# A hybrid attention and mixture-of-experts step: score halves on 64 rows, sampled value products on column groups in turn, page multiplies behind the weight difference

## The chip, the cores and the metric

The kernel runs on one core of one Trainium2 chip. Its time is the device time of one execution in microseconds (us); the metric is the median over the runs. The core has a matrix engine (TensorE, PE in the profile; PEld are its weight loads), VectorE (DVE), ScalarE (ACT), GpSimd (POOL) and SyncE (SP), which here only issues transfers.

## What is computed

One decoder layer over 256 prompt positions and 8 sampled sequences of one token each. Everything is fp32. Cut to what matters here:

```
q, k, v, bg, cg, xc = split(rms_norm(x) @ w_in)        # q, k: 8 heads x 2 halves x 64; v: 8 heads x 128
# prompt, per head h; c is the half of q and k
s[c] = (q[c] . k[c]) * 64**-0.5 - slope[h] * dist       # causal
a = softmax(s[0]) - lam * softmax(s[1]);  o = a @ v     # "the weight difference", then the value product
# sampled tokens: the same against 256 past keys and values, read by page_table (2 pages of 128 x 1024 each)
y_conv = bg * conv3(cg * xc)
x += [rms_norm(o) * (1 - lam_init) | y_conv] @ w_out
x += top-2 experts of 32 (SwiGLU, 2048 -> 512 -> 2048)
```

## The kernel before

**Stages.** First the normed input is multiplied with `w_in` in 48 output tiles of 128 columns (`tile(n)`, 16 products of 128x128 by 128x264 each, L603), then 16 tiles of `w_out`, then the router, then 8 groups of 4 experts. Tile order: 8 of q, 8 of k, 8 of v (n = 0 to 23), then C, X and B of the convolution in turn (n = 24 + 3i is C, + 1 is X, + 2 is B, for i = 0 to 7). Tile n writes PSUM bank n % 3.

**The attention steps lie between the tiles on PE.** Head h has its scores behind tile 18 + 3h (`head_scores`), its three transposes behind tile 19 + 3h (`head_turn`, L652 to L654, which waits for the semaphore `diffed`), its value products behind tile 20 + 3h (`head_pv`). Between scores and transposes stands one tile. In that time DVE adds the bias (`bias_scores`, L1142, L1145), takes the maxima, ACT the exponentials, DVE the output of the head before (`head_out`, L1134) and the difference of the two softmaxes (`difference`, L1157 to L1163), whose last operation counts `diffed` up.

**Scores.** POOL copies the two 64-row halves of q into `qz`, a tile whose other halves are zero (`split_q`, L1454 and L1456), so that each half can be multiplied with all 128 rows of k. `head_scores` then does per half one product of 256 and one of 128 columns, the long ones into bank 5, the short ones into bank 6.

**Sampled tokens.** The key pages are read into the ring (units `KP`, four pages of 512 KB), POOL multiplies each page with the broadcast q (`multiply_page`, L1468, units `QB` hold q), DVE sums it up (`page`, L1129) behind `conv_output(i)`. `PAGES_AT = [3, 3, 3, 3, 2, 2, 0, 0]` says how many pages belong to convolution step i. The value pages (units `VP`, again four pages each) are multiplied behind tile 44 (`sample_pv`, L692), with 32 columns of weights each, so that sample b writes the 32 rows of column group b % 4 of banks 4 and 5.

**Transfers.** `ring` has 8 slots of 2 MB. SP issues the units of `FRONT` in that list's order, each after the work on the unit that held its slot 8 units ago. Near the end of the list stand ("X", 3), ("B", 3), four VP units and eight W units (`w_out`). ("B", 3) takes the slot of the second QB unit and so waits for all 16 page multiplies (`page_mul`); the VP units stand behind it in SP's queue. Behind W come the experts' weights, 12 MB an expert.

**DVE and POOL** both work in SBUF on their own queues, each in program order.

Of the kernel before, what the change touches and what calls it, by code (L numbers as in the profile page):

```python
# [15 lines left out]
ALU = mybir.AluOpType  # L16
# [3 lines left out]
P = 128  # L20
D = 2048
KT = D // P
SEQ = 256
NB = 8
T = SEQ + NB
TT = 3
H = 8
HD = 128
HALF = HD // 2
ATT = H * HD  # L30
CONV = D - ATT
CT = CONV // P
PAST = 256
PAGE = 128
NPG = PAST // PAGE
# [17 lines left out]
C = P // EG  # L53
# [21 lines left out]
BCX = 3 * H  # L75

PAGES_AT = [3, 3, 3, 3, 2, 2, 0, 0]
PAGES_BY = [sum(PAGES_AT[:i]) for i in range(CT + 1)]
NPAGES = NB * NPG
NIN = BCX + 3 * CT  # L80
HEAD0 = 2 * H + 2
# [47 lines left out]
def build(nc, ins, outs):  # L129
    ctx = ExitStack()  # L130
    with ctx:
# [3 lines left out]
        def sem(name):  # L135
            return ctx.enter_context(nc.semaphore(name))

        ring = sb("ring", [P, SLOTS, UNIT])
# [11 lines left out]
        bank = [ctx.enter_context(nc.psum_tensor(f"bank{i}", [P, 512], F32)) for i in range(8)]  # L150
# [19 lines left out]
        qkT = bc[:, KT * T:].rearrange("p (k t) -> p k t", t=T)  # L170
        vrow = xa[:, 0, :].rearrange("p (t c) -> p t c", t=2)
        qrows = xa[0:NB, 0, 0:ATT]
        tmp = xa[:, 1:3, :].rearrange("p a n -> p (a n)")
        prob = tmp[:, 0:768]
        qz = tmp[:, 768:1280].rearrange("p (c q) -> p c q", c=2)
        osq = tmp[:, 1296:1552]
        ord_ = tmp[:, 1560:1816]
        sq = [tmp[:, 1296 + T * i:1296 + T * i + T] for i in range(2)]
# [11 lines left out]
        pairw = tmp[:, 0:512].rearrange("p (g b c) -> p g b c", g=NPG, b=NB)  # L190
# [114 lines left out]
        qk_ready = sem("qk_ready")  # L305
# [9 lines left out]
        stash_T = sem("stash_T")  # L315
        stash_out = sem("stash_out")
        stash_ready = sem("stash_ready")
        qz_ready = sem("qz_ready")
        qz_zero = sem("qz_zero")
        scores = sem("scores")  # L320
        biased = sem("biased")
        exped = sem("exped")
        diffed = sem("diffed")
# [7 lines left out]
        page_mul = sem("page_mul")  # L331
# [8 lines left out]
        s_pv = sem("s_pv")  # L340
# [49 lines left out]
        front_at = {}  # L390
# [155 lines left out]
        def _(pe):  # L546
# [86 lines left out]

            def head_scores(h):

                pe.wait_ge(qz_ready, h + 1)
                if h >= 1:
                    pe.wait_ge(biased, h)
                for c in range(2):
                    pe.matmul(bank[5][:, c * SEQ:(c + 1) * SEQ], qz[:, c, P:SEQ], qkT[:, H + h, 0:SEQ],  # L640
                              start=True, stop=True)
                for c in range(2):
                    m = pe.matmul(bank[6][:, c * P:(c + 1) * P], qz[:, c, 0:P], qkT[:, H + h, 0:P],
                                  start=True, stop=True)
                m.then_inc(scores, 1)

            def head_turn(h):
# [33 lines left out]
            def sample_pv():  # L681

                pe.wait_ge(s_pair_copied, 2)
                pe.wait_ge(rows_out, 3 * H)
                for b in range(NB):
                    u = b // 2
                    if b % 2 == 0:
                        arrived(pe, ("VP", u))
                    for g in range(NPG):
                        page = ((b % 2) * NPG + g) * ATT  # L690
                        for half in range(2):
                            m = pe.matmul(bank[4 + half][C * (b % 4):C * (b % 4 + 1), :], pairw[:, g, b, :],  # L692
                                          ring[:, front_at[("VP", u)][0], page + half * 512:page + (half + 1) * 512],
                                          start=b < 4 and g == 0, stop=b >= 4 and g == NPG - 1, skip_group_check=True)
                    if b % 2:
                        m.then_inc(s_pv, 1)

            def sample_pick():

# [12 lines left out]
            for n in range(NIN):  # L712
# [5 lines left out]
                h, stage = divmod(n - HEAD0, 3)  # L718
# [357 lines left out]
        def _(dve):  # L1076
# [61 lines left out]
            def bias_scores(i):  # L1138

                dve.wait_ge(scores, i + 1)  # L1140
                for c in range(2):
                    st.add(V.scalar_tensor_tensor(prob[:, c * SEQ:(c + 1) * SEQ], const("dist"), SLOPES[i],  # L1142
                                                  bank[5][:, c * SEQ:(c + 1) * SEQ], ALU.mult, ALU.add))
                for c in range(2):
                    st.add(V.scalar_tensor_tensor(prob[:, 512 + c * P:512 + (c + 1) * P], const("dist")[:, P:2 * P], SLOPES[i],  # L1145
                                                  bank[6][:, c * P:(c + 1) * P], ALU.mult, ALU.add))
                st.wait()
                st.do(V.tensor_reduce(nmax[:, 0:2], prob[:, 0:512].rearrange("p (c k) -> p c k", c=2), AX.X, ALU.max, negate=True))
                V.tensor_reduce(nmax[:, 2:4], prob[:, 512:768].rearrange("p (c k) -> p c k", c=2), AX.X, ALU.max, negate=True
                                ).then_inc(biased, 1)  # L1150
# [284 lines left out]
        @block.gpsimd  # L1435
        def _(pool):
            G = nc.gpsimd
            G.memset(xa[:, 2, :], 0.0).then_inc(x_clear, 1)
            pool.wait_ge(x_clear, 1)
            xs = ins["x_sample"].rearrange("b o d -> b (o d)")  # L1440
            pool.dma_start(xa[0:NB, 2, :], xs).then_inc(x_in[2], 16)

            pool.dma_start(outs["conv_sample"][0, :, 0, :], ins["state_conv"][0, :, 1, :]).then_inc(state_stored, 16)


            pool.wait_ge(h_T, KT)
            G.memset(qz, 0.0).then_inc(qz_zero, 1)
            pool.wait_ge(qz_zero, 1)
            def split_q(h):
                pool.wait_ge(qk_ready, h + 1)  # L1450
                if h >= 1:
                    pool.wait_ge(scores, h)

                G.tensor_copy(qz[0:HALF, 0, :], qkT[0:HALF, h, 0:SEQ]).then_inc(qz_zero, 1)  # L1454
                pool.wait_ge(qz_zero, h + 2)
                G.tensor_copy(qz[HALF:P, 1, :], qkT[HALF:P, h, 0:SEQ]).then_inc(qz_ready, 1)  # L1456
                pool.wait_ge(qz_ready, h + 1)

            def multiply_page(j):
                b = j // NPG  # L1460
                if j % PPU == 0:
                    arrived(pool, ("KP", j // PPU))
                if b % 4 == 0 and j % NPG == 0:
                    arrived(pool, ("QB", b // 4))
                s, _ = front_at[("KP", j // PPU)]
                sq_, _ = front_at[("QB", b // 4)]
                kp = ring[:, s, (j % PPU) * ATT:(j % PPU + 1) * ATT]
                G.tensor_tensor(kp, kp, ring[:, sq_, (b % 4) * ATT:(b % 4 + 1) * ATT], ALU.mult).then_inc(page_mul, 1)  # L1468

            for n in range(HEAD0 - 3, NIN, 3):  # L1470

                h, i = (n + 3 - HEAD0) // 3, (n - BCX) // 3
                if h < H:
                    split_q(h)
                if i >= 0:
                    for j in range(PAGES_BY[i], PAGES_BY[i + 1]):
                        multiply_page(j)
                    if PAGES_AT[i]:
                        pool.wait_ge(page_mul, PAGES_BY[i + 1])

            pool.wait_ge(scores, H)
            pool.wait_ge(self_ready, 1)
            G.memset(wrv, 0.0).then_inc(wr_zero, 1)
            G.memset(rbias, FAR).then_inc(wr_zero, 1)
            pool.wait_ge(wr_zero, 2)
            pool.dma_start(wrv[:, :, 0:GROUPS], ins["w_router_group"].rearrange("l (k p) e -> (l p) k e", p=P)).then_inc(wr_in, 16)
            pool.dma_start(wrv[:, :, RG:], ins["w_router_expert"].rearrange("l (k p) e -> (l p) k e", p=P)).then_inc(wr_in, 16)
            pool.dma_start(rbias[:, 0:GROUPS], ins["b_router_group"].partition_broadcast(P).rearrange("p l e -> p (l e)")  # L1490
                           ).then_inc(wr_in, 16)
            pool.dma_start(rbias[:, RG:], ins["b_router_expert"].partition_broadcast(P).rearrange("p l e -> p (l e)")
                           ).then_inc(wr_in, 16)
            pool.wait_ge(wr_in, 64)
            G.tensor_tensor(wrv, wrv, gffnT.unsqueeze(2).to_broadcast([P, KT, RE]), ALU.mult).then_inc(wr_ready, 1)

            pool.wait_ge(o_ready, H + 1)
            G.memset(xa[:, 2, :], 0.0).then_inc(x2_zero, 1)
            pool.dma_start(consts[:, late0:late0 + 512], ins["late"]).then_inc(late_in, 16)

            pool.wait_ge(tile_done, NIN)
            G.memset(h2[:, 2, :], 0.0).then_inc(h2_zero, 1)
            pool.wait_ge(h2_zero, 1)
            for j in range(KT):
                pool.wait_ge(y_added, j + 1)
                cols = slice(j * P, (j + 1) * P)
                G.tensor_copy(h2[:, 0:2, cols], xa[:, 0:2, cols]).then_inc(h2_ready, 1)
                G.tensor_copy(h2[0:NB, 2, cols], xa[0:NB, 2, cols]).then_inc(h2_ready, 1)
# [64 lines left out]
```

## Time and profile before

| | before |
|---|---|
| time, median of 3 runs | 1541.65 us (1540.58 to 1541.82) |
| span of the profiled execution | 1537.7 us |
| what the runs' median has beyond that span | 3.95 us |
| PE busy | 1353.1 us (88%) |
| DVE, ACT, POOL busy | 375.5, 213.2, 67.2 us |
| read from HBM | 496.35 MB |

The span is from the first to the last instruction of one profiled execution. For that execution no time of its own is given beside its span, so the 3.95 us are the difference of two executions. Busy shares are means over stages with different limits.

### The profile page before, as it was taken

How to read it: one execution, taken by the hardware profiler on the slowest of the kernel's cores; microseconds unless marked ns; L12 is line 12 of the kernel's file. 1: busy time of each engine (PE TensorE's matmuls, PEld its weight loads, DVE VectorE, ACT ScalarE, POOL GpSimd, SP SyncE). 2: the span in 40 equal slices, each digit the busy share in tenths (PEclk: the TensorE clock that was granted, in tenths of full speed). 3: DMA queues.
4: the chain of work that ended last, by engine and by line, in shares of the span. 5: the costliest groups of instructions: out<-in, count | busy, mean ns of one | idle time of the engine just before them, and what ended most of it. 6: DMA issues, size and time to landing. Idle time of an engine off the chain costs nothing.

```text
span 1537.7 us, 19543 instructions
## 1 busy us (share of the span) xinstructions
PE 1353.1 (88%) x8104; PEld 912.7 (59%) x8104; DVE 375.5 (24%) x842; ACT 213.2 (14%) x555; POOL 67.2 (4%) x82
## 2 busy tenths in 40 slices
PE   6999999989999987879969879879879878978887
PEld 5888888778687766436426437436535535535542
DVE  3322144644111123113103103203113113112112
ACT  4111231212001120110100100100110110110110
POOL 0000022421010000000000000000000000000000
PEclk9999999989999998879979979889989989988988
DMA  9964334757197432999999999999999999999997
GB/s 299 353 202 175 128 127 144 244 178 243 50 313 268 154 120 101 417 424 423 420 423 423 423 418 424 424 419 422 423 422 418 425 423 418 422 424 422 418 426 294
DMA packets 135644, 503.39 MB, mean 327 GB/s; under 512 B 6214, under 2 KB 80638, under 8 KB 118702
## 3 DMA queue, kind: packets, MB, share of 16 engines
q1 hardware_dynamic: 125670, 495.25, 81.3%
q10 hardware_dynamic: 9600, 6.95, 1.4%
q0 software_dynamic: 336, 0.67, 0.2%
q8 instruction: 26, 0.43, 0.1%
q14 instruction: 12, 0.10, 0.0%
HBM read 496.35 MB, written 6.53 MB: 327 GB/s over the span
## 4 chain that ended last, share of the span: by engine, by line
PE 70%; DMA 17%; DVE 5%; SPq 5%; issue 2%; ACT 1%; ACTq 0%; DVEq 0%
PE bank L603 28%; DMA ring<-in_w_up 13%; PE bank L811 11%; PE bank L798 9%; PE bank L870 7%; PE bank L849 5%; SPq L485 4%; PE bank L834 4%; DMA ring<-in_w_down 2%; DVE bc L1415 1%; PE bank L692 1%; DVE xa L1161 1%; DVE cat L1410 1%; PE bank L754 1%; DMA ring<-in_w_in 1%
## 5 line engine op out<-in xcount | busy, mean ns | idle before, releaser
L603 PE MATMUL bank<-bc,ring 128*128 128x264 f32 x1536 | 353.9, 389 | 1.7 <-DMA ring<-in_w_in 1.7
L798 PE MATMUL bank<-ring,cat 128*32 128x512 f32 x2048 | 270.9, 661 | 82.0 <-DMA ring<-in_w_gate 37.7
L603 PEld LDWEIGHTS bank<-bc,ring 128*128 128x128 f32 x1536 | 290.9, 192 | 52.2 <-DMA ring<-in_w_in 1.9
L870 PE MATMUL bank<-ring,bc 128*32 128x256 f32 x2048 | 174.7, 512 | 33.9 <-DVE bc L1417 28.7
L798 PEld LDWEIGHTS bank<-ring,cat 128*32 128x32 f32 x2048 | 62.1, 116 | 225.6 <-issue 120.1
L811 PEld LDWEIGHTS bank<-bc 128*128 128x128 f32 x768 | 169.4, 311 | 15.1 <-issue 14.1
L849 PEld LDWEIGHTS bank<-consts,bc 128*128 128x128 f32 x512 | 124.3, 327 | 90.3 <-DVE bc L1415 61.0
L811 PE MATMUL bank<-bc 128*128 128x128 f32 x768 | 170.4, 383 | 5.6 <-DVE bc L1379 5.6
L849 PE MATMUL bank<-consts,bc 128*128 128x32 f32 x512 | 131.5, 401 | 26.0 <-DVE bc L1415 26.0
L870 PEld LDWEIGHTS bank<-ring,bc 128*32 128x32 f32 x2048 | 84.8, 144 | 112.1 <-issue 82.1
L603 PE MATMUL bank<-cat,ring 128*128 128x264 f32 x512 | 117.9, 389 | 0.0
L603 PEld LDWEIGHTS bank<-cat,ring 128*128 128x128 f32 x512 | 96.0, 190 | 21.5 <-issue 5.9
L1415 DVE COPY bc<-bank 128x512 f32<-128x512 f32 x32 | 22.1, 692 | 349.2 <-PE bank L798 349.2
L1425 DVE COPY cat<-bank 32x256 f32<-32x256 f32 x128 | 54.3, 424 | 164.3 <-PE bank L870 162.3
L1071 ACT ACTIVATE cat<-bank 32x256 f32<-32x256 f32 x128 | 47.9, 374 | 177.6 <-PE bank L870 176.0
L1410 DVE TENSOR_TENSOR cat<-bank,gains 128x512 f32<-128x512 f32 x32 | 22.1, 692 | 154.1 <-PE bank L811 154.1
L834 PE MATMUL bank<-cat,bc 128*128 128x512 f32 x128 | 59.2, 605 | 0.0
L1431 DVE TENSOR_TENSOR xa<-xa,bank 128x512 f32<-128x512 f32 x72 | 49.5, 688 | 14.7 <-PE bank L834 10.9
L1116 DVE RECIPROCAL xa<-xa 128x264 f32<-128x264 f32 x16 | 28.8, 1803 | 89.9 <-ACT xa L923 89.9
L1064 ACT ACTIVATE bc<-bank 128x128 f32<-128x128 f32 x32 | 8.9, 278 | 288.6 <-PE bank L849 288.6
L834 PEld LDWEIGHTS bank<-cat,bc 128*128 128x128 f32 x128 | 23.0, 189 | 33.0 <-issue 26.3
L1059 ACT ACTIVATE bc<-bank 128x384 f32<-128x384 f32 x8 | 3.9, 491 | 262.3 <-PE bank L822 262.3
(239 smaller groups left out, 640.9 us busy)
## 6 DMA issues: line engine op xcount, KB each, us to landing
ring<-in_w_gate SPq DMA_DIRECT2D x64, 2048.0 KB, 23.6
ring<-in_w_up SPq DMA_DIRECT2D x64, 2048.0 KB, 23.1
ring<-in_w_down SPq DMA_DIRECT2D x64, 2048.0 KB, 27.6
ring<-in_w_in SPq DMA_DIRECT2D x24, 2048.0 KB, 10.6
ring<-in_w_out SPq DMA_DIRECT2D x8, 2048.0 KB, 17.1
ring<-in_cache_k SPq DMA_DIRECT2D x16, 512.0 KB, 4.6
ring<-in_cache_v SPq DMA_DIRECT2D x16, 512.0 KB, 5.3
ring<-qrows_scratch SPq DMA_DIRECT2D x2, 2048.0 KB, 7.3
```

Of the source, the lines that this page charges most:

```text
L485: sp.dma_start(ring[:, s, :], src).then_inc(slot_full[s], 16)
L603: m = pe.matmul(bank[n % 3][:, 0:T], w[:, k, (i % TPU) * P:(i % TPU + 1) * P], src[:, k, :], start=n_k == 0, stop=n_k == KT - 1)
L798: m = pe.matmul(bank[b][c * C:(c + 1) * C, :], xeT[:, 8 * i + k, j * C:(j + 1) * C], w[:, k, :], start=i == 0 and k < 4, stop=i == 1 and k ...
L811: m = pe.matmul(bank[4 + q % 2][:, (k % 4) * P:(k % 4 + 1) * P], h2[:, t, k::KT], sel[:, t, :], start=t == 0, stop=t == TT - 1)
L834: m = pe.matmul(to[:, :], gateT[:, t, :], ye[:, n * 512:(n + 1) * 512], start=True, stop=True)
L849: m = pe.matmul(bank[3][:, (x * FC + c) * C:(x * FC + c + 1) * C], src[:, c::FC], const("fold"), start=True, stop=True)
L870: m = pe.matmul(bank[2 + 2 * i][n * C:(n + 1) * C, 0:256], actT[:, c, :], w[:, c, n, :], start=c == 0, stop=c == FC - 1, skip_group_check= ...
L1071: A(ye[j * C:(j + 1) * C, i * 1024 + n * 256:i * 1024 + (n + 1) * 256], bank[2 + 2 * i][n * C:(n + 1) * C, 0:256], ACT.Copy).then_inc(ye_a ...
L1410: V.tensor_tensor(xeT[:, 4 * q:4 * q + 4, :], bank[4 + q % 2][:, :].rearrange("p (k s) -> p k s", k=4), gffn[:, 4 * q:4 * q + 4].unsqueeze ...
L1415: V.tensor_copy(u_sb, bank[1][:, :]).then_inc(u_copied, 1)
L1425: V.tensor_copy(ye[j * C:(j + 1) * C, i * 1024 + n * 256:i * 1024 + (n + 1) * 256], bank[2 + 2 * i][n * C:(n + 1) * C, 0:256]).then_inc(ye ...
L1431: V.tensor_tensor(xa[:, t, cols], xa[:, t, cols], bank[5 + x % 3][:, :], ALU.add).then_inc(mix_added, 1)
```

## The change

Three edits. In `head_scores` the padded `qz` is gone: each half of q and k is multiplied with its own 64 rows, half c into bank 5 + c (256 columns for the second block of positions, then 128 for the first); POOL's `memset` and 16 copies go with it. In `sample_pv` the samples go in two rounds of four; within a round, page and half are the outer loops and the four samples, hence the four column groups, the inner one; PE waits for two VP units ahead of each round. POOL's page multiplies of step i wait for `diffed` of head i + 2 (at most head 7), where they stood behind `split_q(i + 3)`, which waited for the scores of head i + 2.

```diff
             def head_scores(h):
 
-                pe.wait_ge(qz_ready, h + 1)
+                pe.wait_ge(qk_ready, H + h + 1)
                 if h >= 1:
                     pe.wait_ge(biased, h)
-                for c in range(2):
-                    pe.matmul(bank[5][:, c * SEQ:(c + 1) * SEQ], qz[:, c, P:SEQ], qkT[:, H + h, 0:SEQ],
-                              start=True, stop=True)
-                for c in range(2):
-                    m = pe.matmul(bank[6][:, c * P:(c + 1) * P], qz[:, c, 0:P], qkT[:, H + h, 0:P],
-                                  start=True, stop=True)
+                for q0, q1, b0 in ((P, SEQ, 0), (0, P, SEQ)):
+                    for c in range(2):
+                        half = slice(c * HALF, (c + 1) * HALF)
+                        m = pe.matmul(bank[5 + c][:, b0:b0 + q1], qkT[half, h, q0:q1], qkT[half, H + h, 0:q1],
+                                      start=True, stop=True)
                 m.then_inc(scores, 1)
...
                 pe.wait_ge(rows_out, 3 * H)
-                for b in range(NB):
-                    u = b // 2
-                    if b % 2 == 0:
+                for r in range(2):
+                    for u in (2 * r, 2 * r + 1):
                         arrived(pe, ("VP", u))
                     for g in range(NPG):
-                        page = ((b % 2) * NPG + g) * ATT
                         for half in range(2):
-                            m = pe.matmul(bank[4 + half][C * (b % 4):C * (b % 4 + 1), :], pairw[:, g, b, :],
-                                          ring[:, front_at[("VP", u)][0], page + half * 512:page + (half + 1) * 512],
-                                          start=b < 4 and g == 0, stop=b >= 4 and g == NPG - 1, skip_group_check=True)
-                    if b % 2:
-                        m.then_inc(s_pv, 1)
+                            for x in range(4):
+                                b = 4 * r + x
+                                page = ((b % 2) * NPG + g) * ATT + half * 512
+                                m = pe.matmul(bank[4 + half][C * x:C * (x + 1), :], pairw[:, g, b, :],
+                                              ring[:, front_at[("VP", b // 2)][0], page:page + 512],
+                                              start=r == 0 and g == 0, stop=r == 1 and g == NPG - 1, skip_group_check=True)
+                    m.then_inc(s_pv, 2)
...
-            for n in range(HEAD0 - 3, NIN, 3):
-
-                h, i = (n + 3 - HEAD0) // 3, (n - BCX) // 3
-                if h < H:
-                    split_q(h)
-                if i >= 0:
+            for i in range(CT):
+                if PAGES_AT[i]:
+
+                    pool.wait_ge(diffed, min(i + (BCX - HEAD0) // 3, H - 1) + 1)
                     for j in range(PAGES_BY[i], PAGES_BY[i + 1]):
                         multiply_page(j)
-                    if PAGES_AT[i]:
-                        pool.wait_ge(page_mul, PAGES_BY[i + 1])
+                    pool.wait_ge(page_mul, PAGES_BY[i + 1])
```

On POOL, before, the last copies of q (head 7), the last four page multiplies and the clearing of the router's weights stand so:

```order
L1454 COPY xa<-bc 64x256 [waits scores,qk_ready,page_mul]
L1456 COPY xa<-bc 64x256 [waits qz_zero]
L1468 TENSOR_TENSOR ring<-ring 128x1024 [waits slot_full2,qz_ready]
L1468 TENSOR_TENSOR ring<-ring 128x1024
L1468 TENSOR_TENSOR ring<-ring 128x1024 [waits page_mul]
L1468 TENSOR_TENSOR ring<-ring 128x1024
L1485 MEMSET bc 128x640 [waits self_ready,scores,page_mul]
```

At the same place of the changed kernel:

```order
L1452 TENSOR_TENSOR ring<-ring 128x1024 [waits slot_full2,diffed,page_mul]
L1452 TENSOR_TENSOR ring<-ring 128x1024
L1452 TENSOR_TENSOR ring<-ring 128x1024 [waits diffed,page_mul]
L1452 TENSOR_TENSOR ring<-ring 128x1024
L1466 MEMSET bc 128x640 [waits self_ready,scores,page_mul]
```

All four used to follow the scores of head 6; now the first two follow the difference of head 6 and the last two that of head 7, and the router's clearing stays behind them.

On PE, before, the sampled value products of the first two samples and the first wait of the next two (one row is one product; a product of fp32 is two instructions in the trace):

```order
L692 MATMUL bank4<-ring,xa 32x512 [waits slot_full6,rows_out,s_pair_copied]
L692 MATMUL bank5<-ring,xa 32x512
L692 MATMUL bank4<-ring,xa 32x512
L692 MATMUL bank5<-ring,xa 32x512
L692 MATMUL bank4<-ring,xa 32x512
L692 MATMUL bank5<-ring,xa 32x512
L692 MATMUL bank4<-ring,xa 32x512
L692 MATMUL bank5<-ring,xa 32x512
L692 MATMUL bank4<-ring,xa 32x512 [waits slot_full7]
```

The same stage of the changed kernel, first round and start of the second:

```order
L689 MATMUL bank4<-ring,xa 32x512 [waits slot_full6,slot_full7,rows_out,s_pair_copied]
L689 MATMUL bank4<-ring,xa 32x512 x3
L689 MATMUL bank5<-ring,xa 32x512 x4
L689 MATMUL bank4<-ring,xa 32x512 x4
L689 MATMUL bank5<-ring,xa 32x512 x4
L689 MATMUL bank4<-ring,xa 32x512 [waits slot_full1,slot_full0]
```

Four products with the same bank in a row are those of the four column groups. The last two units (slots 0 and 1) are now waited for together, ahead of the whole second round.

## Rows read from the trace of the kernel before

**Rows 1.** The page, section 2: granted TensorE clock in 40 slices of 38.4 us

```profile
PEclk9999999989999998879979979889989989988988
```

**Rows 2.** Busy time by stretch: us, PE, PEld, DVE, ACT, POOL, PEclk, DMA share, GB/s

```profile
500.00:550.00 50.00, 50.00 (x226) 39.50 (x226) 7.17 (x26) 5.93 (x36) 3.78 (x12) 1.00 0.36 131
700.00:800.00 100.00, 83.34 (x601) 49.72 (x601) 15.24 (x39) 9.38 (x21) 0.00 (x0) 0.90 1.01 421
```

**Rows 3.** The chain that ended last, 272 to 348 us: start, us, what

```profile
272.33 0.75 DVE xa L1142 x2
...
298.55 0.75 DVE xa L1142 x2
...
304.43 2.30 DVE xa L1161
...
308.10 8.81 PE bank L603 x32
...
326.47 0.75 DVE xa L1142 x2
...
338.41 9.26 PE bank L603 x32
```

**Rows 4.** Timeline, 296 to 345 us: start, us, engine line op

```profile
299.61 7.02 POOL L1468 TENSOR_TENSOR ring<-ring 128x1024 f32<-128x1024 f32 x3
...
317.30 3.47 DVE L1129 TENSOR_REDUCE xa<-ring 128x16 f32<-128x1024 f32 x3
...
327.52 9.39 POOL L1468 TENSOR_TENSOR ring<-ring 128x1024 f32<-128x1024 f32 x4
...
334.73 2.46 DVE L1162 SCALAR_TENSOR_TENSOR xa<-xa,small 128x256 f32<-128x256 f32 x1
```

**Rows 5.** Timeline of head 7, for which POOL multiplies no page

```profile
357.22 0.75 DVE L1142 SCALAR_TENSOR_TENSOR xa<-consts,bank 128x256 f32<-128x256 f32 x2 [6.83 <-PE bank L643]
...
362.61 0.28 DVE L1161 TENSOR_SCALAR xa<-xa,small 128x128 f32<-128x128 f32 x1
...
363.32 0.35 DVE L1163 SCALAR_TENSOR_TENSOR xa<-xa,small 128x128 f32<-128x128 f32 x1
364.14 0.27 PE L652 MATMUL bank<-consts,xa 128*128 128x128 f32 x1
```

**Rows 6.** Groups by line, 160 to 425 us: busy, mean ns, idle before

```profile
L652 PE MATMUL bank<-consts,xa 128*128 128x128 f32 x8 | 2.7, 333 | 11.3 <-DVE xa L1163 11.3
```

**Rows 7.** The same chain, 355 to 418 us

```profile
355.87 0.86 PE bank L640 x4
356.74 0.45 PE bank L643 x4
357.18 7.12 PE bank L603 x32
...
379.53 0.43 PE bank L632 x2
...
395.31 15.78 PE bank L692 x64
411.09 7.32 PE bank L603 x32
```

**Rows 8.** The same chain, among the experts

```profile
624.81 5.15 PE bank L798 x48
```

**Rows 9.** Timeline of SP's queue, 336 to 376 us

```profile
336.94 0.37 SPq L473 DMA_DIRECT2D ring<-in_w_in  x1
338.07 38.02 SPq L468 DMA_DIRECT2D ring<-in_cache_v  x16
```

**Rows 10.** Issues at 342.1, 358.4 and 359.5 us: KB, us to landing

```profile
ring<-in_cache_v SPq DMA_DIRECT2D x1, 512.0 KB, 8.0
...
ring<-in_cache_v SPq DMA_DIRECT2D x1, 512.0 KB, 5.1
...
ring<-in_cache_v SPq DMA_DIRECT2D x1, 512.0 KB, 8.5
```

More of the change, by code:

```diff
@@ L174, in build @@
         prob = tmp[:, 0:768]
-        qz = tmp[:, 768:1280].rearrange("p (c q) -> p c q", c=2)
         osq = tmp[:, 1296:1552]
@@ L317, in build @@
         stash_ready = sem("stash_ready")
-        qz_ready = sem("qz_ready")
-        qz_zero = sem("qz_zero")
         scores = sem("scores")
@@ L1142, in bias_scores @@
                     st.add(V.scalar_tensor_tensor(prob[:, c * SEQ:(c + 1) * SEQ], const("dist"), SLOPES[i],
-                                                  bank[5][:, c * SEQ:(c + 1) * SEQ], ALU.mult, ALU.add))
+                                                  bank[5 + c][:, 0:SEQ], ALU.mult, ALU.add))
                 for c in range(2):
                     st.add(V.scalar_tensor_tensor(prob[:, 512 + c * P:512 + (c + 1) * P], const("dist")[:, P:2 * P], SLOPES[i],
-                                                  bank[6][:, c * P:(c + 1) * P], ALU.mult, ALU.add))
+                                                  bank[5 + c][:, SEQ:SEQ + P], ALU.mult, ALU.add))
                 st.wait()
@@ L1446, in _ @@
             pool.wait_ge(h_T, KT)
[L1447 to L1457, printed above, removed]
             def multiply_page(j):
```

## The prediction

> **What bounds the kernel now.** I read the busy time by stretch first, then the chain of waits, then the timeline of one head with page multiplies and of one without. Late in the program the transfers bound it: from 700 to 800 us the DMA share is 1.01 at 421 GB/s. From 500 to 550 us, while `w_out` is multiplied, PE is busy for all 50 us and the DMA share is 0.36 [rows 2]: the ring is full of expert weights, and the stream goes on only when the first experts free slots. The chain up to there runs through PE. So what PE (or what PE waits for) saves ahead of the experts starts the saturated stream earlier by as much, and I count it in full.
>
> In that front part the chain leaves PE once per head: PE has done the tile behind the scores and waits at L652 for DVE's last operation of the difference, 11.3 us in all [rows 6]. The reader should set two heads side by side. In the head at 298.55, POOL multiplies three pages from 299.61 to 306.6, and DVE's small L1161 takes 2.30 us in the chain [rows 3, 4]. In head 7 POOL multiplies none, L1161 takes 0.28, and from the first bias (357.22) to the end of L1163 (363.67) DVE needs 6.45 us; PE's tile takes 7.12, and L652 starts at 364.14 without a wait [rows 5, 7]. The last head with pages has four of them, and there L1162 takes 2.46 too [rows 4]. So some DVE operations stand still until a page multiply (2.34 to 2.35 us each, 7.02 over 3 and 9.39 over 4) is done.
>
> **Page multiplies behind the difference.** The distance of one head's scores from the next is 26.22 us at 272.33, 27.92 at 298.55 and 30.75 at 326.47 (to 357.22) [rows 3, 5]; the two heads before repeat the first. Without pages it is 24.09: from 357.18 to the end of the sums at 379.96, plus the 1.31 us of scores [rows 7]. Five heads: 3 x 2.13 + 3.83 + 6.66 = 16.9, less 0.3 for transposes of v that one of them has between its tiles: 16.5 us. Part of it is clock: after the waits at heads 5 and 6 a tile took 8.81 and 9.26 us where 7.12 is usual [rows 3, 7], in the slice where the page shows 8 tenths [rows 1]; 3.8 of the 16.5 hang on that, and they come back only if PE no longer idles. DVE has then 0.4 us to spare per head (363.67 against 364.14), so this term rests on a thin cover.
>
> What is late instead: the multiplies now lie over DVE's convolution step, which can be held until the last of three is done, 7.1 us after the difference, or 6.45 + 7.1 = 13.6 us after the scores, plus the operations themselves, some 2 us more. The product with B needs its tile anyhow, two tiles of 7.12 and 0.3 of transposes, 14.6 us after the scores. With the multiplies' end at 15.6, 0.4 for that product and 3.5 for the page sums (3.47 us for three [rows 4]) DVE is free 19.5 us after the scores, and the next scores come at 23.7. Cost 0; without this cover every us beyond the spare 4.2 would be paid once per head.
>
> **The moved transfers.** This is the price. All 16 multiplies used to be done 10 us after the scores of head 6 (at 336.9), and ("B", 3) was issued at 336.94 with the 16 value pages behind it [rows 4, 9]. Now the last two wait for head 7: 6.45 + 2 x 2.35 = 11.2 us after its scores; counted from the old 357.2 that is 368.4, 31.5 us later than 336.94. POOL's router loads wait behind them and fall into the same stretch. When are the value pages wanted? The products started 38.1 us after head 7's scores (357.18 to 395.31) [rows 7]; the second round begins 3.5 us later, so the last pages are due 41.6 - 11.2 = 30.4 us after ("B", 3) is issued. Before, the fourth page, issued at 342.1, landed 8.0 later [rows 10], 13.2 after that issue with 4.2 MB moved. Twelve pages (6.3 MB) more take 15.0 us at 421 GB/s [rows 2] or 19.8 at the pace of those 13.2: 28.2 to 33.0. The router's loads cost a page 8.5 against 5.1 us when they were issued beside it [rows 10], so 3.4 more: 31.6 to 36.4, a wait of 1.2 to 6.0 us. I take 3, nearer the quick end since a queue that never runs dry should hold its pace, and 1 more for the clock, about half of the 2.1 us that the tile at 338.41 lost. Cost 4. ("B", 3) itself is due at tile 44, some 20 us after its issue, and lands in time.
>
> **Value products in turn.** Now 64 instructions take 15.78 us, 247 ns each [rows 7]: one column group gets eight in a row, and only neighbours overlap. The experts' L798 has the new order with the same shape: 48 in 5.15 us, 107 ns each [rows 8]. So 64 x 0.107 = 6.9, with 0.2 for the start 7.1: 8.7 saved.
>
> The Trainium skill ("TensorE: Matmul & The Clock Gate", Part 3, what overlaps and what doesn't) has matmuls start and end in strict program order. With the two passes of each fp32 product adjacent, that allows only one overlap per neighbouring pair and would leave this stage near 14 us. The trace speaks against it, since L798 could not then reach 107 ns.
>
> **Scores on 64 rows.** Now 0.86 + 0.45 = 1.31 us per head [rows 7]. The new products have the same columns, twice 256 and twice 128. Side by side on the two row halves they take half, 0.65; one after the other 1.31. No row of this trace shows a product on 64 rows. To this comes the change of array shape, twice a head: the tile behind the 32-column stage took 7.32 instead of 7.12 [rows 7], so 0.2 for one change; I take 0.3 for the two. Bounds: 0.36 saved per head, or 0.3 lost. The nearest rows are the column groups, which do run side by side, so I take the gain: 8 x 0.36 = 2.9 saved, the other end being 2.4 lost. POOL's copies stood beside other work and PE never waited for them: 0.
>
> The skill's page "TensorEngine Tiling (Array Packing)" (Key Properties) says that changing the tiling mode drains TensorE, and that tiles work independently. The 0.2 us of the trace are what such a drain costs here; by that page the sum would be the same.
>
> **Sum.** 16.5 + 8.7 + 2.9 - 4 = 24.1. The span goes from 1537.7 to 1513.6; with the 3.95 us that the median has beyond it, 1517.5.
>
> **Rivals.**
> - No wait for the value pages (0.25): the queue holds 421 GB/s and the router's loads cost less than 3.4. 28.1 saved, 1513.5. For it: the quick bound misses by only 1.2 us.
> - Row halves in sequence, with the wait (0.16): 24.1 - 5.3 = 18.8, 1522.8. For it: no row shows them side by side.
> - A long wait for the pages, 6 us and a slow clock behind it (0.08): about 9 for 4, 19, 1522.5; at the far end 1526. For it: the slow pace in [rows 10].
> - Products in program order (0.04): the value stage saves 1.7, the scores 0.16 a head, which is 1.3, and with the second round so much later the pages are in time: 16.5 + 1.7 + 1.3 = 19.5, 1522.1. This is the rule of the skill named above. Against it: [rows 8].
> - The port wait isn't POOL's doing and stays (0.02): 16.5 fall away and the pages' lateness too; the rest, with serial row halves, is 8.7 - 2.4 = 6.3, 1535. Against it: head 7.
> - Slower (0.03): DVE, held in the convolution step, is late for the next head's bias. Place: five heads. Price: 1 us per head and us beyond the spare 4.2. It takes back all 28.1 us only from 4.2 + 28.1 / 5 = 9.8 us of extra hold on; three multiplies are 7.1 us. At 12 us it gives 1541.65 - 28.1 + 5 x 7.8 = 1552.5.
> - What is left, 0.42, is the forecast.
>
> **How the numbers follow.** 1517.5 is the likeliest case. Its own uncertainty is the wait (0 to 9) and the 0.2 us per change of shape. The range, 1510 to 1526, holds the forecast, no wait and the three cases near 1522; the low end is no wait with cheaper changes of shape, 30.5 saved being 1511. A run can tell 0.2% or 3 us from no change, and all but the last two cases are beyond that: faster 0.95, same 0.02, slower 0.03.
>
> **What would show it.** In the profile after: L1161 at 0.28 us in all heads and no idle time before the transposes; distances between scores of 23.7 us; no tile at 8.8 or 9.3 us there; the value products near 7 us with a gap of about 3 us in their middle that ends with a DMA of `cache_v`; the eight score groups at 0.65 to 0.7 us and the tile behind each some 0.2 longer; held DVE operations in L1174 to L1178 instead. A wait before ("B", 3)'s tile, a gap of more than 9 us among the value products, or idle time that stays before the transposes would make the prediction wrong.

## The result, and the profile after

| | before | changed |
|---|---|---|
| time, median of 4 runs | 1541.12 us (1540.55 to 1541.82) | 1517.74 us (1515.57 to 1518.75) |
| span of the profiled execution | 1537.7 us | 1515.5 us |
| that execution's own time | not given | 1517.3 us |
| PE busy | 1353.1 us | 1340.8 us |
| DVE, POOL busy | 375.5, 67.2 us | 388.9, 60.4 us |

The ratio is 0.9847, with a 95% interval from 0.9835 to 0.986: the changed kernel is 1.5% faster, 23.4 us by the medians and 22.2 us by the spans.

The chain that ended last, in the changed kernel (start, us, what), answers to [rows 3] and [rows 7]. L639 is the 64-row scores, L648 the first transpose, L600 the tiles, L689 the sampled value products.

```profile
243.40 7.32 PE bank L600 x32
250.72 0.11 PE bank L648
...
267.23 7.32 PE bank L600 x32
...
337.86 0.88 PE bank L639 x8
338.76 0.75 DVE xa L1138 x2
...
347.68 2.40 POOL ring L1452
350.10 0.37 SPq L470
...
369.02 14.61 DMA ring<-in_cache_v
383.63 0.14 issue
383.77 5.34 PE bank L689 x32
389.11 7.32 PE bank L600 x32
```

Where DVE stood between scores and transposes of the heads with pages, the chain now runs from tile to transpose without leaving PE. Behind head 7's scores it leaves PE by another way: through DVE's bias and difference, the last page multiplies on POOL (L1452), the issue of ("B", 3) (L470) and of the value pages behind it, to the landing of the last page, for which the second round of value products waits. The scores come every 23.83 us (243.40 to 267.23) where it was 26.22 to 30.75. Head 7's scores are done at 338.76, 18.4 us earlier than at 357.18, and the tile behind the value products starts at 389.11 instead of 411.09: 22.0 us. The span's gain is 22.2, so behind that point nothing is won or lost, and the saturated stream of expert weights takes over as much earlier. In nine of the ten experiments below the two gains, against the same trace of before, also agree within 0.7 us; with the values alone they are 9.3 and 7.4.

Groups by line, 160 to 425 us, of the changed kernel (busy, mean ns, idle before):

```profile
L1171 DVE TENSOR_SCALAR xa<-small 128x8 f32<-128x8 f32 x8 | 14.3, 1791 | 0.0
L1172 DVE SCALAR_TENSOR_TENSOR xa<-xa,small 128x256 f32<-128x256 f32 x8 | 12.1, 1507 | 0.3
L689 PE MATMUL bank<-ring,xa 128*32 128x512 f32 x64 | 9.0, 711 | 3.2 <-DMA ring<-in_cache_v 3.2
L1157 DVE TENSOR_SCALAR xa<-xa,small 128x128 f32<-128x128 f32 x8 | 2.2, 280 | 0.0
L648 PE MATMUL bank<-consts,xa 128*128 128x128 f32 x8 | 2.2, 279 | 0.1
```

The idle time ahead of the transposes is 0.1 us in place of 11.3 [rows 6]. The difference's L1157 (L1161 before) takes 280 ns in the mean. What POOL holds back are now operations of the convolution: L1171 writes 8 columns and takes 1.8 us. DVE is busy for 13 us more and the kernel is faster all the same, since PE waits for none of them. And L689 has a wait of 3.2 us for value pages.

The timeline of PE around that wait, and the busy time by stretch through it (PEclk is the third value from the end):

```profile
376.97 3.64 PE L689 MATMUL bank<-ring,xa 128*32 128x512 f32 x32
383.77 5.34 PE L689 MATMUL bank<-ring,xa 128*32 128x512 f32 x32 [3.16 <-DMA ring<-in_cache_v]
```

```profile
380.50:383.70 3.20, 0.11 (x4) 0.00 (x0) 0.00 (x0) 0.00 (x0) 0.00 (x0) 1.00 1.07 363
383.80:386.80 3.00, 3.00 (x20) 1.06 (x24) 0.00 (x0) 0.00 (x0) 0.00 (x0) 0.64 1.08 341
```

The first round of 32 instructions is over in 3.6 us, the second needs 5.3: behind the wait the granted clock is 0.64 in the mean over 3 us, so for most of that stretch it is the lower of the two levels (1.2 GHz, where the other is 2.4).

### The profile page after: what moved, and what is told of

Read it like the earlier page. It is cut to its first block, busy times and chain, and to the rows that moved or that the text cites. A ratio compares the mean times of both kernels' runs of the same rounds, so it can differ in the third digit from the quotient of the medians.

```text
span 1515.5 us, 19525 instructions
## 1 busy us (share of the span) xinstructions
PE 1340.8 (88%) x8104; PEld 907.2 (60%) x8104; DVE 388.9 (26%) x842; ACT 212.9 (14%) x555; POOL 60.4 (4%) x65
## 4 chain that ended last, share of the span: by engine, by line
PE 69%; DMA 19%; SPq 5%; DVE 4%; issue 2%; ACT 1%; POOL 0%; ACTq 0%; DVEq 0%; POOLq 0%
PE bank L600 28%; PE bank L807 11%; PE bank L794 10%; DMA ring<-in_w_down 10%; DMA ring<-in_w_up 7%; PE bank L866 7%; PE bank L845 5%; PE bank L830 4%; SPq L482 4%; DMA ring<-in_cache_v 1%; DVE bc L1411 1%; DVE cat L1406 1%; DMA xa<-in_x_prompt 1%; PE bank L750 1%; PE bank L834 1%
## 5 line engine op out<-in xcount | busy, mean ns | idle before, releaser
L600 PE MATMUL bank<-bc,ring 128*128 128x264 f32 x1536 | 350.8, 387 | 0.0
L794 PE MATMUL bank<-ring,cat 128*32 128x512 f32 x2048 | 266.0, 652 | 77.5 <-DMA ring<-in_w_gate 36.0
L600 PEld LDWEIGHTS bank<-bc,ring 128*128 128x128 f32 x1536 | 288.2, 190 | 50.0 <-issue 0.8
L866 PE MATMUL bank<-ring,bc 128*32 128x256 f32 x2048 | 180.1, 523 | 37.9 <-DVE bc L1413 28.7
L600 PE MATMUL bank<-cat,ring 128*128 128x264 f32 x512 | 117.9, 389 | 0.0
L600 PEld LDWEIGHTS bank<-cat,ring 128*128 128x128 f32 x512 | 96.0, 190 | 21.5 <-issue 5.9
L1411 DVE COPY bc<-bank 128x512 f32<-128x512 f32 x32 | 22.1, 692 | 337.8 <-PE bank L794 337.8
L1406 DVE TENSOR_TENSOR cat<-bank,gains 128x512 f32<-128x512 f32 x32 | 22.1, 692 | 155.8 <-PE bank L807 155.8
L1427 DVE TENSOR_TENSOR xa<-xa,bank 128x512 f32<-128x512 f32 x72 | 49.5, 688 | 14.7 <-PE bank L830 11.3
L1452 POOL TENSOR_TENSOR ring<-ring 128x1024 f32<-128x1024 f32 x16 | 37.5, 2370 | 308.5 <-DVE xa L1159 308.5
## 6 DMA issues: line engine op xcount, KB each, us to landing
ring<-in_w_gate SPq DMA_DIRECT2D x64, 2048.0 KB, 23.4
ring<-in_cache_v SPq DMA_DIRECT2D x16, 512.0 KB, 12.4
```

The lines of the kernel that those rows point to most:

```text
L600: m = pe.matmul(bank[n % 3][:, 0:T], w[:, k, (i % TPU) * P:(i % TPU + 1) * P], src[:, k, :], start=n_k == 0, stop=n_k == KT - 1)
L794: m = pe.matmul(bank[b][c * C:(c + 1) * C, :], xeT[:, 8 * i + k, j * C:(j + 1) * C], w[:, k, :], start=i == 0 and k < 4, stop=i == 1 and k ...
L866: m = pe.matmul(bank[2 + 2 * i][n * C:(n + 1) * C, 0:256], actT[:, c, :], w[:, c, n, :], start=c == 0, stop=c == FC - 1, skip_group_check= ...
L1406: V.tensor_tensor(xeT[:, 4 * q:4 * q + 4, :], bank[4 + q % 2][:, :].rearrange("p (k s) -> p k s", k=4), gffn[:, 4 * q:4 * q + 4].unsqueeze ...
L1427: V.tensor_tensor(xa[:, t, cols], xa[:, t, cols], bank[5 + x % 3][:, :], ALU.add).then_inc(mix_added, 1)
```

## The experiments

Each ran beside the kernel before on the same chip. Ratios are to that kernel, with their 95% intervals. Three chips were used: the kernel before took 1541.65 us beside the first four rows, 1540.01 beside the next four and 1541.57 beside the last two. The changed kernel's 1517.74 us were measured apart from them, so a difference of medians from it can be off by 1 to 2 us, and where less is at stake the traces decide.

| run | median us | span | ratio |
|---|---|---|---|
| pages alone | 1523.25 | 1521.4 | 0.9887 (0.9871 to 0.9904) |
| values alone | 1532.45 | 1530.3 | 0.9949 (0.9932 to 0.9966) |
| scores alone | 1531.52 | 1529.9 | 0.9937 (0.9921 to 0.9954) |
| last pages early | 1512.9 | 1510.5 | 0.9819 (0.9803 to 0.9836) |
| router late | 1512.6 | 1510.9 | 0.9821 (0.9804 to 0.9837) |
| same row half | 1522.87 | 1521.3 | 0.9888 (0.9871 to 0.9904) |
| runs of four | 1517.29 | 1515.3 | 0.985 (0.9834 to 0.9867) |
| longer hold | 1516.37 | 1513.7 | 0.9848 (0.9831 to 0.9864) |
| both moves | 1513.06 | 1511.1 | 0.9817 (0.9804 to 0.983) |
| pages behind bias | 1530.15 | 1527.7 | 0.9937 (0.9922 to 0.9952) |

### Page multiplies behind the difference, alone

On the kernel before:

```diff
                 if i >= 0:
+                    if PAGES_AT[i]:
+                        pool.wait_ge(diffed, min(i + (BCX - HEAD0) // 3, H - 1) + 1)
                     for j in range(PAGES_BY[i], PAGES_BY[i + 1]):
                         multiply_page(j)
```

> The kernel before with the third edit alone: page multiplies wait for the weight difference, padded scores and the old order of the value products stay. My theory: the idle time before the transposes goes, 11.3 us to 0, and with it the slow tiles behind heads 5 and 6; the scores of head 7 come 16.5 us earlier; the value products in their old order want the last pages 50 us after head 7's scores and so don't wait for the later transfers. 16.5 saved, 1524.6. Rival: the later value pages cost here too, a wait of 3 us or more in the value products, 1528 or above. Second rival: the waits move into the convolution step and come back at the next head, less than 10 saved.

Its chain:

```profile
340.52 0.44 PE bank L643 x4
340.96 7.12 PE bank L603 x32
...
379.10 15.78 PE bank L692 x64
394.88 7.32 PE bank L603 x32
```

Head 7's scores end at 340.96, 16.2 us earlier, against the 16.5 forecast. The value products in their old order run through without a wait although their pages are as late as in the changed kernel. 16.2 us are saved in the chain, 16.3 by the spans and 18.4 by the medians (15 to 20 by the ratio's interval); the first theory holds, both rivals fall.

### The value products in turn, alone

`sample_pv` of the changed kernel in the kernel before.

> The kernel before with the new order of the sampled value products alone. All value pages have landed 13 us before the stage begins, so it should run without a gap: 64 instructions at 107 ns, 7.1 us instead of 15.8. 8.7 saved, 1532.4. If matmuls had to start in program order the stage would take about 14 us and 1.7 would be saved, 1539.4.

Its chain:

```profile
394.79 7.00 PE bank L693 x64
401.80 7.32 PE bank L603 x32
```

7.00 us in place of 15.78, 109 ns per instruction, and no gap: 8.8 saved by the stage, 7.4 by the spans and 9.2 by the medians. Matmuls that start in strict program order are ruled out. The single records of the changed kernel's trace show it too: the first instructions of four column groups start 6 to 7 ns apart, and the second one of the first product, which stands ahead of three of them in the program, 0.45 us later.

### The 64-row scores, alone

`head_scores` and `bias_scores` of the changed kernel, and on POOL, in place of `split_q` and its order:

```diff
-                    pool.wait_ge(diffed, min(i + (BCX - HEAD0) // 3, H - 1) + 1)
+                    pool.wait_ge(scores, min(i + (BCX - HEAD0) // 3, H - 2) + 1)
```

> The kernel before with the 64-row scores alone: no padded q, page multiplies directly behind the scores of the same head as before (without POOL's two copies of 0.9 us ahead of them), value products in the old order. The matmuls alone give 0.26 us a head (0.46 shorter scores, 0.2 longer next tile), 2.1 in all: 1539.0. My theory adds that the multiplies start 0.9 us earlier against DVE's difference, so each of the five held heads is released up to 0.9 us earlier: 4 more, 1535. If that second part is absent, 1539.

7.8 us by the spans, 10.1 by the medians: more than either number. One held head of its timeline, and the group of its waits:

```profile
244.94 6.99 POOL L1452 TENSOR_TENSOR ring<-ring 128x1024 f32<-128x1024 f32 x3 [18.07 <-PE bank L639]
...
249.95 2.13 DVE L1156 TENSOR_SCALAR xa<-xa,small 128x256 f32<-128x256 f32 x1
252.00 0.27 DVE L1157 TENSOR_SCALAR xa<-xa,small 128x128 f32<-128x128 f32 x1
```

```profile
L648 PE MATMUL bank<-consts,xa 128*128 128x128 f32 x8 | 2.5, 314 | 7.1 <-DVE xa L1159 6.9
```

Without the two copies POOL is done at 251.9, 7.1 us after the scores instead of 8.0, and DVE's difference is let go earlier: 7.1 us idle instead of 11.3 (4.2), and the tile behind head 5's transposes back at 7.12 us instead of 8.81. Head 6's is at 8.81 instead of 9.26, so 2.1 of clock. With 2.1 of shorter scores that is 8.4, near the span's 7.8. My second part was right in kind; I had left out the clock. In the changed kernel this gain isn't to be had a second time, since there the waits are gone anyway.

### The last page multiplies one head earlier

On the changed kernel:

```diff
-                    pool.wait_ge(diffed, min(i + (BCX - HEAD0) // 3, H - 1) + 1)
+                    pool.wait_ge(diffed, min(i + (BCX - HEAD0) // 3, H - 2) + 1)
```

> The changed kernel, but the last two page multiplies wait for the difference of head 6 instead of head 7, so that the last of the input weights and the value pages are issued some 20 us earlier. My theory: the gap of 3.2 us in the middle of the value products goes and with it the slow clock in their second round (5.3 to 3.5 us); head 7 isn't held, since DVE is free 2 us before its scores. 5 saved against the changed kernel, 1512.7. Rival: four multiplies in one convolution step (9.4 us) hold DVE past the scores of head 7, and what is gained is lost there: 1516 to 1518.

Its chain:

```profile
337.69 0.85 PE bank L639 x8
...
376.87 7.00 PE bank L689 x64
```

The gap and the slow clock are gone, head 7 is as early as in the changed kernel, and the tile behind the stage starts at 383.88 instead of 389.11, 5.2 us earlier; 5.0 by the spans, 4.8 by the medians. Four multiplies in one step do no harm.

### The router loads behind the value products

On the changed kernel, in POOL's code ahead of clearing `wrv`:

```diff
             pool.wait_ge(scores, H)
+            pool.wait_ge(s_pv, 4)
             pool.wait_ge(self_ready, 1)
```

> The changed kernel, but POOL issues its four router loads only behind the sampled value products. My theory: these loads of small pieces cost the weights and pages in flight 3.4 us; without them the last value page lands some 3 us earlier, the gap of 3.2 us shrinks to under 0.5 and the second round runs at full clock: 4 to 5 saved, 1513. Rival: the gap is the bandwidth of 10.5 MB behind a late issue, whatever else runs: it stays at 3 us, 1517.7.

The chain through the stage, and the landing of ("B", 3), issued at 350.1, and of the last value page, issued at 369.0 and 368.7; first the changed kernel, then this one:

```profile
ring<-in_w_in SPq DMA_DIRECT2D x1, 2048.0 KB, 12.1
...
ring<-in_cache_v SPq DMA_DIRECT2D x1, 512.0 KB, 14.6
```

```profile
376.99 7.00 PE bank L689 x64
383.99 7.32 PE bank L600 x32
...
ring<-in_w_in SPq DMA_DIRECT2D x1, 2048.0 KB, 8.1
...
ring<-in_cache_v SPq DMA_DIRECT2D x1, 512.0 KB, 11.4
```

306 KB of router weights, biases included, keep 2 MB in flight 4 us longer, and the last page lands 3.5 us later (369.02 + 14.6 against 368.73 + 11.4). That is all of the 3.2 us gap. The rival, bandwidth alone, falls: without them the pages land at 380.1, just ahead of the second round. The edit also moves POOL's clearing of `wrv` (under 1 us) back; no run separates it from the loads.

### Both halves of the scores on the same rows

On the changed kernel; the second half of q and k is left out and the first is used twice:

```diff
-                        m = pe.matmul(bank[5 + c][:, b0:b0 + q1], qkT[half, h, q0:q1], qkT[half, H + h, 0:q1],
+                        m = pe.matmul(bank[5 + c][:, b0:b0 + q1], qkT[0:HALF, h, q0:q1], qkT[0:HALF, H + h, 0:q1],
```

> The changed kernel, but both halves of the scores are multiplied on rows 0 to 63 (the second half of q and k is left out and the first used twice), so nothing can run side by side. If the two row halves do run side by side in the changed kernel, a head's scores go from 0.85 to about 1.4 us, 0.6 x 8 = 4.6 us slower than the changed kernel, 1522.3. If they don't, the time is the same, 1517.7. The tile behind the scores stays at 7.32 in both.

```profile
244.06 1.50 PE bank L639 x8
245.56 7.32 PE bank L600 x32
```

1.50 us a head in place of 0.85, 8 x 0.65 = 5.2 us; the tile behind the value products starts 4.9 us later (394.02), and the medians differ by 5.1. So the two row halves do run side by side, and without that the edit would be slower than the padded scores: 1.50 + 0.20 against 1.31. This run leaves half of q and k out, so its output isn't the layer's; it stands for its time alone.

### Four instructions in a row for one column group

On the changed kernel:

```diff
-                        for half in range(2):
-                            for x in range(4):
-                                b = 4 * r + x
+                        for x in range(4):
+                            b = 4 * r + x
+                            for half in range(2):
```

> The changed kernel, but in each round a sample's two halves stand next to each other, so that four instructions in a row go to one column group (two in the changed kernel, eight in the kernel before). Theory A: TensorE looks only some four matmuls ahead, so about two groups overlap: 200 to 220 ns per instruction, 13 to 14 us for the stage, no wait for pages in the middle; 1.5 us slower than the changed kernel, 1519. Theory B: it looks far enough to use all four groups: 107 ns, the same time as the changed kernel.

```profile
377.09 3.68 PE L689 MATMUL bank<-ring,xa 128*32 128x512 f32 x32
383.49 5.36 PE L689 MATMUL bank<-ring,xa 128*32 128x512 f32 x32 [2.72 <-DMA ring<-in_cache_v]
```

3.68 us for the first round against 3.64: theory B. Four in a row lose nothing, eight in a row lose half. Both agree with four instructions waiting per column group and the fifth blocking those behind it: with eight in a row the next sample starts with the fifth, so 8 x 4 + 4 = 36 steps of 429 ns, 15.4 us, where 15.78 were measured. The single records of the kernel before agree: the second sample's first instruction starts 1.75 us behind the first sample's, 6 ns behind that sample's fifth. That picture fits the three orders that were run (two, four and eight in a row); five to seven in a row were not tried.

### More work on POOL in the convolution step

On the changed kernel, behind each step's page multiplies, on a spare tile that nothing reads:

```diff
                     pool.wait_ge(page_mul, PAGES_BY[i + 1])
+                    for x in range(6):
+                        G.tensor_tensor(spare, spare, spare, ALU.mult).then_inc(spare_sem, 1)
+                        n_spare[0] += 1
+                        pool.wait_ge(spare_sem, n_spare[0])
```

> The changed kernel with six more multiplies of 128x512 on a spare tile behind the page multiplies of each step (work that nothing uses), about 7 us more of POOL per step for six steps. It measures the cover of the convolution step: DVE is free 19.5 us after the scores and the next come at 23.8, so 4.3 us are spare. If held operations add all 7 us, DVE is 2.7 us late at each of five heads: 13 us slower, 1531. If DVE needs only one slot between two multiplies and gets through its few held operations early, the cost is near 0 and the time 1518 to 1520.

```profile
274.25 7.03 POOL L1457 TENSOR_TENSOR ring<-ring 128x1024 f32<-128x1024 f32 x3 [9.96 <-DVE xa L1161]
...
281.36 6.77 POOL L1467 TENSOR_TENSOR xa<-xa 128x512 f32<-128x512 f32 x6
281.49 1.00 DVE L1175 SCALAR_TENSOR_TENSOR xa<-small,xa 128x8 f32<-128x8 f32 x1
282.52 1.35 DVE L1176 SCALAR_TENSOR_TENSOR xa<-xa,small 128x264 f32<-128x264 f32 x1
...
285.05 3.46 DVE L1127 TENSOR_REDUCE xa<-ring 128x16 f32<-128x1024 f32 x3
```

With 6.8 us more of POOL in a step the scores still come every 23.83 us. The median of 1516.4 lies even below the forecast's 1518 to 1520: here the second round of value products, after a wait of 2.63 us, ran at the full clock (3.64 us instead of 5.34). A held DVE operation waits for one POOL operation, not for POOL to fall idle, and the page sums (L1127) aren't held at all: three take 3.46 us beside POOL as they took 3.47 with POOL idle [rows 4]. "All 7 us are added" was wrong.

### Page multiplies between bias and difference

On the changed kernel:

```diff
-                    pool.wait_ge(diffed, min(i + (BCX - HEAD0) // 3, H - 1) + 1)
+                    pool.wait_ge(biased, min(i + (BCX - HEAD0) // 3, H - 1) + 1)
```

> The changed kernel, but the page multiplies wait for the bias of the same head (the maxima, 2.4 us after the scores) instead of the difference, so they lie over the rest of DVE's chain again. My theory: DVE's last four operations of the difference wait for the ends of multiplies, the last at 9.5 us after the scores, the difference ends at 10 to 10.5 where the tile ends at 7.3: some 3 us idle at each of five heads and slow tiles behind them, against 5 us gained at the value products, since the last pages come 4 us earlier: 1525 to 1535. Rival: any place behind the bias is as good as behind the difference, since DVE slips through between two multiplies: 1513.

```profile
280.10 2.16 DVE xa L1156
282.26 2.29 DVE xa L1157
```

```profile
L648 PE MATMUL bank<-consts,xa 128*128 128x128 f32 x8 | 2.7, 339 | 14.8 <-DVE xa L1159 14.7
```

The two scalings of the difference stand for 4.5 us again, PE idles 14.8 us, and the kernel is 12.4 us slower than the changed one, in the forecast range. So the third edit's gain is its place, behind the difference. That `split_q` no longer stands ahead isn't what brings it: with pages alone `split_q` stayed and 16.2 us were saved, and with the scores alone it went and 7.1 of the 11.3 us idle remained.

### Both moves together

The wait of the early last pages and that of the late router loads in one kernel.

> The changed kernel with both moves: the last two page multiplies behind the difference of head 6, and the router loads behind the value products. Each alone took the gap away and brought the stage to 7.0 us, so together they should give no more than either: 1512.7. Were there a second cost of either lateness that the stage doesn't show, it would be faster than both, 1511 or less.

1513.06, against 1512.9 and 1512.6, and the stage takes 7.00 us: nothing on top. All three beat the changed kernel by 4.7 to 5.1 us by the medians, by 5.1 to 5.2 at the start of the tile behind the stage, and can't be told from each other. The last pages one head earlier is the better choice of the two moves: a change of one number, and it leaves the value pages 13 us of reserve (the last one lands at 363.9, the stage starts at 376.87), where the late router loads leave about none.

## Why the prediction was right

**The carry-over into the expert stage** held: 22.0 us at the end of the front part, 22.2 by the spans.

**Page multiplies behind the difference**: 16.5 forecast, 16.2 measured alone. The transposes' idle time, the slow tiles and the place where the hold reappears (the convolution step) came out as written, with L1157 at 280 ns. The hold there cost 0, as forecast, but for more reasons than I gave: my cover of 4.2 us assumed that each DVE operation might wait until POOL is done, and the longer hold showed that it doesn't. The thin cover of 0.4 us ahead of the transposes was enough.

**The moved transfers**: a wait of 3 us forecast, 3.2 measured, for the clock 1 forecast and 1.8 measured (5.3 against 3.5 us). 4 forecast, 5.0 in all: the clock's share was the mis-sized part. The parts of the estimate were near as well: ("B", 3) was issued 11.3 us after head 7's scores (11.2), and the router's loads cost 3.5 (3.4).

**Value products in turn**: 8.7 forecast, 8.8 measured alone. What the Trainium skill says under "TensorE: Matmul & The Clock Gate", Part 3, strict program order at the start, doesn't hold here: 109 ns per instruction were measured.

**Scores on 64 rows**: 2.9 forecast, 2.1 to 2.2 measured. The products take 0.85 us and the next tile 0.20 longer, 0.26 saved a head instead of 0.36: side by side was right, and the two changes of array shape cost 0.4 instead of 0.3. That tile's 0.20 us agree with the drain at a change of tiling mode that the Trainium skill's "TensorEngine Tiling (Array Packing)" names under Key Properties.

**The sum**: 16.2 + 8.8 + 2.1 - 5.0 = 22.1 where I had 24.1: 0.3 less for the pages' place, 0.8 less for the scores, 1.0 more for the late transfers. By the traces the gain was 2 us too large. That the time still came out at 1517.7 is owed to the other number, the 3.95 us between span and median. They are no property of the kernel: in all four runs of the changed kernel what lies outside the span is 1.8 to 1.9 us, and a run of the kernel before beside one of the experiments, with the same span of 1537.7, took 1539.56. So the execution whose trace I read was most likely 2 us faster than the median of its runs; over all comparisons they range from 1538.94 to 1542.41. To add 3.95 to a span is to take the gain from the medians, and by the medians the gain was 23.4 us (21.6 to 25.4 by the interval), which holds both 22.1 and 24.1. That the forecast is off by only 0.2 us is therefore partly luck; that it lies in the range isn't.

**The rivals.** No wait for the pages (1513.5) was near: it is what the kernel does when either move is made, at 1512.6 to 1512.9. Serial row halves cost 5.1 by the medians and 4.9 in the trace, near the 5.3 forecast. The wait was 3.2 us and not 6, so the long wait didn't occur, and the port wait was POOL's doing, since it went with POOL's place (11.3 us idle to 0.1). Program order and the slower case didn't occur either, and for the latter the longer hold removed the mechanism.

## What to carry to other kernels

When DVE and POOL both work in SBUF, look for DVE operations that last many times their usual length and end with one of POOL's; move POOL's work to a stretch where DVE's result isn't awaited. When a wait is added to free a chain, follow everything that counts on the delayed work: here the last of 16 value pages, behind a weight load in SP's queue, landed 3.2 us too late, and to move either the page multiplies or another engine's small loads out of the way was enough to bring it in in time. For small matmuls on column groups, order so that at most four instructions in a row go to one group: two and four lost nothing here, eight lost half.

## What the runs showed of the hardware

- DVE operations with two SBUF inputs, and scalings in SBUF of 8 columns and more, wait for the running POOL multiply: up to 2.5 us where they take 0.2 to 0.5. So did a copy of 10 columns (0.90 instead of 0.18 us in the longer hold). A reduce from SBUF (L1127, 1.15 us each), operations with a PSUM input (L1138, L1167) and scalings of one column didn't wait. The wait is for one POOL operation, so short POOL operations (1.06 us each) held DVE for 0.9 to 1.35 us. The Trainium skill's "GPSIMD Engine Reference", Key points, names contention with DVE instructions in a 2-port perf mode or with two SBUF inputs. The second kind is what the traces show (L1162 before, 2.46 us); in which mode the held scalings ran, no trace here says.
- 3.2 to 3.7 us without matmuls were followed by half clock for part of the next round (5.0 to 5.4 instead of 3.6 us; granted clock 0.55 to 0.65 over its first 3 us), 2.6 us in the longer hold were not (3.64, clock 1.00). At 2.7 us (runs of four, 5.36, clock 0.65) it did fall; the two waits, 2.63 and 2.72 us, are so close that the runs don't show whether the length alone decides.
- A head's four products of 64 rows, two on either row half, take 0.85 us where the same four on one half take 1.50, so fp32 products run side by side in row halves as they do in column groups.
